# The output stage's DeltaNet half, begun in the tail of the RWKV scan

## What is computed

```
for i in range(DEPTH):                                   # DEPTH = 2
    h = h + 0.5 * g1 * swiglu(modulate(rms_norm(h), ...), ffn_w13[i, 0], ffn_w2[i, 0])
    mix_ctx, mix_lat = token_mixing(...)                 # below
    h_lat = h_lat + m_lat[5] * mix_lat                   # context tokens too, except in the last layer
    h = h + 0.5 * g3 * swiglu(...)

# token mixing: two halves of 512 features, side by side, times w_out (1024 x 1024)
dn = o * rsqrt(mean(o * o)) * w * silu(z)                # DeltaNet heads, done before the RWKV scan
y  = y_forward + y_backward + bonus                      # RWKV-7 heads, two scans
yc = y - mean(y)                                         # per head of 64 features
rw = (yc * rsqrt(mean(yc * yc) + 64e-5) * weight + bias) * gate,   gate = sigmoid(lg) @ g2
out = concatenate([dn, rw]) @ w_out
```

## Time and profile before

| | us |
|---|---|
| median of three runs | 4044.11 |
| lowest, highest | 4041.28, 4049.51 |
| profiled execution, whole | 4048.02 |
| its span in the trace | 4046.3 |
| PE busy | 3823.4 (94%) |
| DVE busy | 2205.7 (55%) |
| ACT busy | 1453.4 (36%) |
| POOL busy | 757.2 (19%) |

### The profile page before, as it was taken

One profiled execution on the slowest core, in us unless ns is written; L12 is line 12 of the kernel. 1 busy time (PEld: TensorE's weight loads), 2 busy tenths in 40 slices (PEclk: granted clock), 3 DMA queues, 4 the chain that ended last, 5 costly groups with the idle time before them and its releaser, 6 DMA issues. The chain is left out here.

```text
span 4046.3 us, 93176 instructions
## 1 busy us (share of the span) xinstructions
PE 3823.4 (94%) x40271; PEld 3339.7 (83%) x40271; DVE 2205.7 (55%) x3770; ACT 1453.4 (36%) x2510; POOL 757.2 (19%) x879
## 2 busy tenths in 40 slices
PE   7999999999988889999999999999999978889999
PEld 5899997878867767999998999987887857757887
DVE  4655556466464444755557555566565464444444
ACT  4322334343353333433234323343343253333222
POOL 1222210043023310222211222200232043300000
PEclk8999999999999999999999999999999989999999
DMA  6433332100200011333223333332000200032232
GB/s 213 126 118 106 104 106 70 47 3 2 81 5 4 5 70 42 112 95 93 84 75 112 108 104 104 110 104 58 22 2 21 66 2 4 4 110 81 86 112 65
DMA packets 409036, 287.20 MB, mean 71 GB/s; under 512 B 13438, under 2 KB 366180, under 8 KB 408164
## 3 DMA queue, kind: packets, MB, share of 16 engines
q1 hardware_dynamic: 408676, 281.86, 22.8%
HBM read 270.27 MB, written 11.53 MB: 70 GB/s over the span
## 5 line engine op out<-in xcount | busy, mean ns | idle before, releaser
L799 ACT ACTIVATE w_hi<-w_raw 128x512 fp32r<-128x512 f32 (+1 forms) x724 | 405.1, 612 | 649.0 <-POOL w_raw L783 348.0
L806 DVE TENSOR_TENSOR w_lo<-w_raw,w_hi 128x512 fp32r<-128x512 f32 (+1 forms) x724 | 484.2, 708 | 174.1 <-ACT w_hi L799 174.1
L914 PE MATMUL PS<-x_hi,w_hi 128*128 128x384 f32 x1680 | 562.4, 335 | 0.7 <-DVE hid_flat L1101 0.7
L914 PE MATMUL PS<-x_lo,w_hi 128*128 128x384 f32 x1680 | 561.3, 334 | 0.0
L914 PE MATMUL PS<-x_hi,w_lo 128*128 128x384 f32 x1680 | 561.2, 334 | 0.0
L1186 DVE SCALAR_TENSOR_TENSOR arena<-PS,mod,arena 128x256 f32<-128x256 f32 (+1 forms) x336 | 198.2, 631 | 331.6 <-PE PS L927 331.4
L1101 DVE TENSOR_TENSOR hid_flat<-hid_flat,PS 128x384 f32<-128x384 f32 (+1 forms) x454 | 245.6, 556 | 237.6 <-PE PS L914 153.6
L927 PE MATMUL PS<-hidden_hi,w_hi 128*128 128x256 f32 (+1 forms) x1232 | 342.0, 347 | 7.6 <-DVE hidden_lo L1153 5.7
L927 PE MATMUL PS<-hidden_hi,w_lo 128*128 128x256 f32 (+1 forms) x1232 | 337.0, 343 | 0.0
L927 PE MATMUL PS<-hidden_lo,w_hi 128*128 128x256 f32 (+1 forms) x1232 | 337.0, 343 | 0.0
L776 POOL TENSOR_TENSOR w_raw<-w_raw 128x512 f32<-128x512 f32 x60 | 85.3, 1421 | 1268.9 <-DMA w_raw<-in_ffn_w_dram 1184.4
(11 more groups left out here) (359 smaller groups left out, 7407.4 us busy)
## 6 DMA issues: line engine op xcount, KB each, us to landing
w_raw<-in_ffn_w_dram SPq DMA_DIRECT2D x512, 256.0 KB, 4.0
arena<-in_ada_w_dram SPq DMA_DIRECT2D x120, 512.0 KB, 5.8
arena<-in_w_in_dram SPq DMA_DIRECT2D x64, 512.0 KB, 3.9
arena<-in_ada_w_dram SPq DMA_DIRECT2D x6, 2048.0 KB, 14.2
arena<-in_w_out_dram SPq DMA_DIRECT2D x16, 512.0 KB, 4.5
h_save<-arena SPq DMA_DIRECT2D x16, 384.0 KB, 2.6
arena<-h_save SPq DMA_DIRECT2D x2, 3072.0 KB, 15.2
w_raw<-in_ffn_w_dram SPq DMA_DIRECT2D x32, 128.0 KB, 2.3
```

Of the source, the lines that this page charges most:

```text
L799: nc.scalar.activation(w_hi[:, high_place(n, what, j), 0:size], w_raw[:, load_of[what] % 2, place, 0:size], ACT.Copy).then_inc(w_high_read ...
L806: nc.vector.tensor_tensor(w_lo[:, b, place, 0:size], w_raw[:, b, place, 0:size], w_hi[:, high_place(n, what, j), 0:size].bitcast(F32), ALU ...
L914: mm = pe.matmul(PS[:, 4 * b + bank, 0:half], w[wo], x_split[xo][:, j, k, 0:half], start=(k == 0 and q == 0), stop=(k == KH - 1 and q == 2))
```

## The change

The program between the scan and the output stage is rearranged in both layers.

- SP's first four loads of the output stage (two tiles of `w_out`, `mix_dn`, `h`) no longer wait for the phase: they wait for POOL's last copy of the scan (`rw_copied`). The two weight tiles have a new place (`first_wout`), so that tiles 2 and 3 of `w_out` are loaded at once when the phase has begun. To make room, `KD` and `KK` of the scan are shifted by 768 columns, and two small scratch tiles (the second `X_PAIRS`, the masks) move.
- In the scan's last full step ACT splits the two weight tiles between its moves. In the last step, which is now `last_step` on PE, ACT splits the four DeltaNet tiles after `move_u` and before `move_out`; DVE makes the low parts of both after its last work in the scan. The low parts of k = 0 to 3 overwrite `mix_dn`.
- PE computes `tiles(0)` between `new_values` and `state_on_r`, and `tiles(1)` to `tiles(3)` behind `values_on_r`, all before it ends the phase.
- In the output stage the four gates are computed first, between the head sums, and ACT copies each to `mix_rw` in SBUF, where DVE's gating reads it. Sums over heads use two pairs of PSUM banks instead of four, since banks 0 to 3 hold the sums of output tiles 0 and 1.
- The spread of the norm has two places (`GO_PLACE`), so that the spread of j + 1 need not wait for the gating of j.

Nothing is computed that was not computed before, except the eight copies of gates per layer on ACT (two for each j).

```diff
-        KD = [region(23808, NB, T), region(26880, NB, T)]
-        KK = region(29952, NB, T)
+        KD = [region(24576, NB, T), region(27648, NB, T)]
+        KK = region(30720, NB, T)
...
+            def last_step(c):
+                new_values(c)
+                pe_out_tiles(pe, layer, 0)
+                state_on_r(c, False)
+                values_on_r(c)
+                for k in range(1, NB):
+                    pe_out_tiles(pe, layer, k)
...
                     move_kb(d, 0)
+                    if d == RW_CHUNKS - 1:
+                        act_out_weights(act, layer, 0)
                     move_y(d, 3)
                     move_kb(d, 1)
+                    if d == RW_CHUNKS - 1:
+                        act_out_weights(act, layer, 1)
+                else:
+                    for k in range(NB):
+                        act_out_high(act, layer, k)
...
+            for t in range(2):
+                dve_out_weights(dve, layer, t)
+            for k in range(NB):
+                dve_out_low(dve, layer, k)
...
+            sp.wait_ge(rw_copied, (COPIES * RW_CHUNKS + ZEROED + WAYS) * (layer + 1))
             load(0)
             load(1)
             sp.dma_start(mix_dn[:, :, :].rearrange("p a b -> p (a b)"), mix_save).then_inc(h_loaded, 16)
             sp.dma_start(h[:, :, :].rearrange("p a b -> p (a b)"), h_save).then_inc(h_saved, 16)
+            dma_after(sp, start_of(layer, 7))
             for t in range(2, KT):
+                if t >= 4:
+                    sp.wait_ge(low_split, SPLIT0 + layer * SPLITS + SPLIT_W[t - 2] + 1)
                 load(t)
...
+            def take_gate(j):
+                bank_ = 4 + 2 * (j % 2)
+                act.wait_ge(go_summed, s0 + GATED[j])
+                sc.activation(mix_rw[:, j, 0:CTX], PS[:, bank_, 0:CTX], ACT.Copy)
+                sc.activation(mix_rw[:, j, CTX:T].rearrange("p (r c) -> p c r", r=GRID_H),
+                              PS[:, bank_ + 1, 0:SEQ].rearrange("p (c r) -> p c r", r=GRID_H), ACT.Copy).then_inc(go_act, 1)
...
+            gate(0)
+            gate(1)
+            average(0)
+            average(1)
+            gate(2)
+            gate(3)
+            average(2)
+            average(3)
...
+            spread(0)
+            spread(1)
             for j in range(NB):
-                pe.wait_ge(go_act, a0 + NB + 2 + j)
-                if j > 0:
-                    pe.wait_ge(go_step, d0 + 13 + 2 * j)
-                else:
-                    pe.wait_ge(go_step, d0 + 13)
-                for t in range(T // P):
-                    mm = pe.matmul(RSTD[:, t * P:(t + 1) * P], gsq[:, j % 2, t * P:(t + 1) * P], ident[:, :], start=True, stop=True)
-                mm.then_inc(go_summed, 1)
...
+                pe_out_tiles(pe, layer, NB + j)
+                if j + 2 < NB:
+                    spread(j + 2)
```

## The result

| | before | after |
|---|---|---|
| median of the runs made together, us | 4042.70 (4035.79 to 4049.51) | 4073.53 (4067.87 to 4074.92) |
| ratio of the two, 95% interval | | 1.0074 [1.0061, 1.0087] |
| profiled execution, us | 4048.02 | 4067.87 |

The change makes the kernel 0.74% slower, some 30.8 us, where the forecast was +4.5 with a range up to 4059 us for the kernel. The two traces differ by 19.9 us only: the profiled execution of before is one of its longer ones, that of after the shortest. So I compare the traces by stages, not by their ends. Each output stage with the scan's tail ahead of it is cut at five events that both kernels have: POOL's last work; the end of DVE's last subtraction in the scan (L2873 before, L2893 after); the first `add`; the end of the inversion; DVE's first move of output tile 0 (L3120, L3193).

What follows compares the result with a forecast made beforehand. PE, busy 94% of the span, was taken as the bound, with gains only where it idles or waits. Terms -2.6 + 1.9 + 0.8 + 3.5 + 1.0 gave +4.6 us; for the median 4044.1 + 4.5 = 4048.6, range 4040 to 4059.

Steps and rivals of the forecast that it cites:

- sum at full clock, both layers: Scan end through output stage, PE at full clock: -0.55 us in layer 0, -2.05 in layer 1, together -2.6.
- ACT's gate copies, through (a): ACT's copies write with a 64-column stride, felt through the head sums: 0 to +1.8 us over two layers, +0.8 taken.
- (a): Chain from first `add` to inversion, head sums now behind gates and copies: +1.2 us in layer 0, +0.5 in layer 1.
- strided gating: DVE's gating reads the gate in SBUF with a 64-column stride: 0 to +3.8 us over eight gatings, +1.9 taken.
- half clock: PE falling to 1.2 GHz after new idles: one spell per layer, +3.5 us, bounds 0 and +8 (two in each).
- early loads, up to the last subtraction: Loads beside the scan's tail: nobody waits for them, path cost 0; instruction fetches under them +1.0 us, bounds 0 and +12.
- The rival: Bulk loads in the tail hold up PE's instructions: 6 us per layer, 12 in all, 4059.6; chance 0.20, 0.15 of it slower.
- `tiles(0)` cannot fill the gap: Last scan step: its low part isn't ready for the 0.71 us gap, so `state_on_r` starts 4.0 us later.
- the phase ends 10 and 6.4 us later: Last scan step: DeltaNet products before the phase's end delay the first `add` by 9.95 us in layer 0, 6.4 in layer 1.
- (b): From inversion to first spread, DeltaNet products gone, only 1.0 us left: -7.0 us in layer 0, -4.0 in layer 1.
- products for nothing in the tail: Faster rival: PE does the DeltaNet products in scan gaps, the phase ends as now, 4032 us; chance 0.05.
- The signs named in advance: Trace checks: first `add` at 1490.9 and 3567.1; wrong if before 1487 or 1448-1464 issue waits grew over 3 us.

Runs made afterwards that it cites:

- hold: The changed kernel plus idle PE products in its gaps (before the first DeltaNet product, the first spread, and RWKV tiles 0 to 2): median 4065.25 us, ratio 1.0044.
- gaps: The changed kernel with the 48 DeltaNet products moved from the scan's tail into PE's gaps behind the spreads, loads and splits left in the tail: 4044.81 us, 1.0006.
- loads_only: The kernel before with only the four early loads and the shifted memory places they need: 4058.34 us beside 4046.19 for before, 1.0031.
- late_gaps_again: Changed kernel, DeltaNet products in the gaps, loads and splits back behind the phase; a repeat for comparison: 4030.41 us, 0.9966 of before.

## Why the prediction was wrong, step by step

The forecast was +4.6 us between traces; in the stretches it was 24.0. By its own terms (the half clock is the surplus over the steps of the forecast; idle products on PE won 12.5 of its 14.7 back, and whether the other 2.2 are clock or an error of the sum isn't shown):

| term | forecast | measured |
|---|---|---|
| sum at full clock, both layers | -2.6 | as forecast, to about 2 us (`hold`) |
| ACT's gate copies, through (a) | +0.8 | +0.8 (2.5 in (a) for 1.7; not isolated) |
| strided gating | +1.9 | 0 |
| half clock | +3.5, bounds 0 and +8 | +14.7 |
| early loads, up to the last subtraction | +1.0, bounds 0 and +12 | +11.1, half clock in the tail included |
| sum | +4.6 | +24.0 |

- **The early loads** are the first failed step: "Cost on the path 0", and +1.0 for the fetches. The tail got 5.2 and 5.9 us longer. The rival priced this at +12 and got 0.20. I had its evidence in hand: 5.9 us of issue waits in the costliest group with empty DMA engines, which, if they are fetches, were not hidden even then. The argument against it, that a block takes only 1.1 us of an engine, proved nothing: the blocks still take about that (1.4% of 16 x 18 us over four is 1.0), and PE still waited longer; that they came late because of the bulk ahead of them is the likely reason, and not shown. The rule of the Trainium skill, "Runtime: NRT & Kernel Launch", section Instruction fetch mechanics, that fetching is mostly hidden, doesn't agree with stops of 2.84 and 3.95 us, if they are fetches. What the Trainium skill, "DMA: Bandwidth & Descriptors", section Queues, rings and completion order, says of engines taking queues in turn fits in so far as four instruction blocks did come in beside the bulk; no run here shows the turns.
- **The mechanism of the rival was only half of it.** Issue waits grew by 2.4 and 4.0 us, the tail by 5.2 and 5.9. Behind the stops there is half clock, in layer 0 from 1462 to 1468 and in layer 1 from 3554 to 3562, in stretches that had 1.00 before. The rest is there: from POOL's end to the last subtraction PE was busy for 24.9 us in place of 22.1 in layer 0, with the same 857 products in both traces, and for 24.0 in place of 22.2 in layer 1, at a mean clock of 0.89 in place of 1.00; 2.8 and 1.8 us that with the waits make up the 5.2 and nearly the 5.9. So a stop could cost twice here, once for itself and once for the clock; the first one, 2.84 us at 1456, had no half clock behind it.
- **The clock** is the second failed step. I took one spell per layer, at most two, from the idles of 2.4 to 4.7 us. There were five per layer, one of them in the tail. To the first `add` it cost 1.5 in each layer (11.42 for 9.95, 7.94 for 6.4), from the first spread on 5.1 and 6.5 us. The idles were forecast about right (2.4 forecast, 2.52 measured before `tiles(0)`; 4.7 and 3.6 forecast, 3.65 each measured, the first shorter only because the spreads ahead of it were slow). What was wrong was to price them by "not every such idle is followed by it", read from a trace in which two of six idles of 2.25 to 2.52 us ahead of tiles 4 to 6 were; of the six longer ones in their place, 3.38 to 4.56 us, five were. Nor did I list the idle of 1.52 ahead of the first spread.
- **The stride**: L3165, which reads and writes with it, takes 1.08 to 1.09 us for the 1.07 of the earlier trace rows. The bound of 0 was right, the middle wrong.
- **Right**: that `tiles(0)` cannot fill the gap, because its low part is not ready; that the phase ends 10 and 6.4 us later (11.4 and 7.9 with the clock); (a) +1.2 and +0.5 (1.6 and 0.9); (b) -7.0 and -4.0 (1.02 from inversion to spread in both layers). But the reason given for the smaller (a) of layer 1, that its 20.92 "already has a spell of half clock in it", doesn't part the layers: layer 0 has one too (0.50 from 1484); in layer 1 it began about 1 us earlier in the chain, and DVE's first centring waited 1.30 us in place of 0.54. The products that left the output stage came back whole ahead of the phase's end, as said.
- **The rival "products for nothing in the tail"** was refuted with the phase's end. Its idea was right in another place: in the gaps of the output stage the same products cost little (`gaps`: 28.37 and 24.99 us behind the inversion, 1.3 more in each layer than `hold`, which has idle products there and none of these).
- **The signs named in advance**: first `add` at 1498.04, not 1490.9; issue waits to 1464 up by 2.8 us (5.6 for 2.8 counting 1448 to 1464), just below my limit of 3, though the fetch rival was true. The limit was set too high, since it left out what the clock adds.

## What to carry to other kernels

Bulk loads are not free because nobody waits for them: before they are moved beside a stretch of many small instructions, look for "issue" waits there, and expect the loads to lengthen them and to bring half clock behind them (here 3.4 and 3.0 us of waits became 6.8 and 7.6 in `loads_only`, and the tails 13.3 us longer); small pieces issued one by one cost the tail a tenth as much here. A dependent chain gains from fewer waits only if work fills the idle time: ahead of a phase's end the 48 products put the first `add` 16.7 us later over both layers (after against `gaps`), behind the spreads they cost about 3, and six idle products ahead of a short idle went with a trace that has no half clock behind the scan. When idles of PE become longer or more frequent, the rate at which the old trace had half clock behind them is no guide: here it went from two of six to five of six as these idles grew from about 2.4 to about 3.7 us, and the upper bound should have a spell behind each.

## What the runs showed of the hardware that was not expected

- Four DMAs of 5.6 MB beside the scan cost 12.2 us, by stops of PE of up to 3.95 us in which it waits for nothing that the trace names. With 4.5 MB of it in twelve pieces, one at a time, the tail paid 0.85 and 0.57 us in place of 6.4 and 6.9.
- The longest of these stops parts the same group of 32 products behind the 30th with and without the loads (1.48 us before, 3.95 in `loads_only`, 4.75 in `gaps`; over all traces 1.2 to 1.5 without and 2.6 to 4.8 with them): it belongs to a place in PE's program, and it is longer when the DMA engines carry bulk beside it.
- Half clock (0.50, 1.2 GHz) came after idles of only 1.51 and 1.52 us ahead of the first spreads, in a chain in which PE had been idle several times for about 1 us; in another execution of the same kernel (`late_gaps_again`), and in layer 1 of after, it didn't come there. After an idle of 3.65 us it failed to come once.
- Outside the stretches that were changed, executions of these kernels differ by up to 19 us; the shortest and the longest of 28 runs of the kernel before lie 22 us apart (4033.5 and 4055.8), more than most of the effects in this study.
